# Third block of a fused network: conv sum split in two, and splits and value products reordered on VectorE and ScalarE

## The reference, cut to what matters

```python
z = rms_norm_2(x, mix_norm_g[l]) @ w_in[l]
(q, kc, vc, ks, vs, kw, vw, gl, zg, zc) = _split_cols(z, IN_SPLITS)
y_nsa = nsa_mixer(q, kc, vc, ks, vs, kw, vw, gl, cmp_pe[l], cmp_w1[l], cmp_w2[l])
y_gmlp = gmlp_mixer(zg, gmlp_ln_g[l], gmlp_ln_b[l], gmlp_ws[l], gmlp_bs[l])
y_conv = conformer_conv_mixer(zc, conv_dw_w[l], conv_dw_b[l], conv_ln_g[l], conv_ln_b[l])
...
y = jnp.concatenate([rms_norm_2(y_nsa, g_nsa), rms_norm_2(y_gmlp, g_gmlp),
                     rms_norm_2(y_conv, g_conv)], axis=-1)
x = x + y @ w_out[l]
```

## Time and profile before

| what | value |
|---|---|
| median of 3 runs | 944.64 us (944.25 to 947.62) |
| time of the profiled execution | 944.2 us |
| its span on the core | 942.5 us |
| PE busy | 896.2 us (95%) |
| DVE busy | 639.0 us (68%) |
| ACT busy | 469.8 us (50%) |
| POOL busy | 166.8 us (18%) |
| mean granted clock | 0.993 |

### The profile page before, as it was taken

How to read it: one execution, slowest core, us unless ns; L and a number is a source line. 1 busy time by engine, 2 the same in 40 slices (tenths; PEclk the granted TensorE clock), 3 DMA queues, 4 the chain that set the end, 5 groups by cost and what they waited for, 6 DMA issues and landing times.

```text
span 942.5 us, 15274 instructions
## 1 busy us (share of the span) xinstructions
PE 896.2 (95%) x5692; PEld 806.4 (86%) x5692; DVE 639.0 (68%) x948; ACT 469.8 (50%) x734; POOL 166.8 (18%) x131
## 2 busy tenths in 40 slices
PE   4999999999998999999999999989999989999996
PEld 4888888888997888888888999978798889999995
DVE  3897777776555678777678687966653676656655
ACT  4854444444545565444444635435543564555442
POOL 2200000000000000000000579102000264444441
PEclk9999999999999999999999999979999999999999
DMA  9777666643431557666674764211444486656601
GB/s 304 210 204 206 192 201 195 188 153 116 151 136 46 164 179 238 201 186 188 186 221 135 175 178 156 90 46 67 134 179 134 126 254 201 191 178 172 196 23 45
DMA packets 187172, 154.27 MB, mean 164 GB/s; under 512 B 6337, under 2 KB 172445, under 8 KB 187117
## 3 DMA queue, kind: packets, MB, share of 16 engines
q1 hardware_dynamic: 185517, 149.19, 52.2%
q0 software_dynamic: 752, 2.39, 1.0%
q10 hardware_dynamic: 848, 1.92, 0.6%
HBM read 151.92 MB, written 1.05 MB: 162 GB/s over the span
## 4 chain that ended last, share of the span: by engine, by line
PE 78%; DVE 10%; ACT 5%; issue 3%; DMA 2%; POOL 2%; SPq 0%; DVEq 0%; ACTq 0%
PE bank L1722 16%; PE bank L1724 16%; PE bank L1723 16%; PE bank L1850 16%; PE bank L1852 8%; DVE wl L991 3%; ACT wh L562 2%; DMA raw<-in_pool_w 1%; PE bank L1814 1%; PE bank L1739 1%; DVE yc L1342 1%; PE bank L2339 1%; POOL st L1617 1%; DVE xhl L1000 1%; PE bank L2318 1%
## 5 line engine op out<-in xcount | busy, mean ns | idle before, releaser
L1850 PE MATMUL bank<-xhl,wh 128*128 128x512 f32 x672 | 235.0, 394 | 0.6 <-DVE wl L991 0.6
L1852 PE MATMUL bank<-xhl,wl 128*128 128x256 f32 x672 | 186.3, 277 | 0.0
L1850 PEld LDWEIGHTS bank<-xhl,wh 128*128 128x128 f32 x672 | 126.0, 187 | 29.9 <-DVE wl L991 0.8
L1722 PE MATMUL bank<-xhl,wh 128*128 128x256 f32 (+1 forms) x520 | 147.9, 285 | 0.8 <-DVE xhl L1250 0.7
L1724 PE MATMUL bank<-xhl,wl 128*128 128x256 f32 (+1 forms) x520 | 146.9, 283 | 0.0
L1723 PE MATMUL bank<-xhl,wh 128*128 128x256 f32 (+1 forms) x520 | 146.9, 283 | 0.0
L991 DVE TENSOR_TENSOR wl<-raw,wh 128x2048 fp32r<-128x2048 f32 (+5 forms) x53 | 114.0, 2160 | 45.1 <-ACT wh L562 45.0
L630 ACT ACTIVATE wh<-raw 128x2048 fp32r<-128x2048 f32 x57 | 109.2, 1916 | 55.8 <-PE bank L1852 52.4
L1852 PEld LDWEIGHTS bank<-xhl,wl 128*128 128x128 f32 x672 | 126.2, 188 | 1.8
L1617 POOL TENSOR_SCALAR st<-ss 128x1 f32<-128x1 f32 x18 | 10.9, 606 | 580.4 <-ACT junk L571 580.2
L1722 PE MATMUL bank<-dh,hh 128*128 128x512 f32 x264 | 103.5, 392 | 5.5 <-DVE hl L1111 5.5
(11 more groups left out here) (304 smaller groups left out, 1712.6 us busy)
## 6 DMA issues: line engine op xcount, KB each, us to landing
raw<-in_ffn_w_up SPq DMA_DIRECT2D x88, 512.0 KB, 6.0
draw<-in_ffn_w_down SPq DMA_DIRECT2D x66, 512.0 KB, 3.6
raw<-in_ffn_w_gate SPq DMA_DIRECT2D x44, 512.0 KB, 5.2
raw<-in_w_in SPq DMA_DIRECT2D x18, 512.0 KB, 4.8
raw<-in_xattn_wk SPq DMA_DIRECT2D x8, 512.0 KB, 4.6
raw<-in_mla_w_o SPq DMA_DIRECT2D x8, 512.0 KB, 4.1
raw<-in_xattn_wv SPq DMA_DIRECT2D x8, 512.0 KB, 4.6
raw<-in_w_out SPq DMA_DIRECT2D x8, 512.0 KB, 4.1
```

What stands on the lines that cost most here:

```text
L1722: pe.matmul(outp, a_hi, b_hi, start=start, stop=False, **kw)
L1850: pe.matmul(b[:, :].rearrange("p (a s) -> p a s", a=2), wh[ns][:, a:a + P], xhl[:, :, k, :], start=k == 0, stop=False, skip_group_check=True)
L1852: ins = pe.matmul(b[:, 0:SEQ], wl[ns][:, a:a + P], xh[:, k, :], start=False, stop=k == KD - 1, skip_group_check=True)
```

## The change

- The region of overlaid tiles grows by 608 bytes, and a tile `yd` (128x256) is new.
- DVE's taps 18 to 30 of row 1 go into `yd` instead of `yc[:, 1, :]`. Tap 18 is a multiply alone, and no longer waits for POOL. A new instruction, `conv_join`, adds `yd` to `yc[:, 1, :]` when both sums are complete, and TensorE's turn of `yc` waits for one more signal.
- The stretches of taps are cut at other places: `conv(26, 33)` for `conv(26, 30)`, `conv(33, 34)` for `conv(30, 31)`, `conv(34, 39)` for `conv(31, 36)`, `conv(39, 44)` and the join for `conv(36, 44)`.
- DVE does `vbd` ahead of these last taps, and the split of `wout2` behind the four gate products of gMLP (L1478).
- ACT copies `kcm` ahead of its rounding of `wout2`, and rounds `wout3` behind `nsa_pt(5, 1)`.
- DVE does `comp_add(1)` behind the four scalings, and the split of `wout3` behind the four tile splits.

```diff
-        REGION = 58688
+        REGION = 59296
...
+        yd = at_("yd", [P, SEQ])
...
             nsa_exp(3, 1)
-            after("z_u")
             act.wait_ge(cmp_mm, 2)
             act.wait_ge(kcm_zero, 1)
             for g in range(GROUPS):
                 rows_ = slice(g * DH, (g + 1) * DH)
                 ins = act.activation(kcm[rows_, g, :], bank[2][rows_, 64:64 + NCMP], ACT.Copy, scale=0.5)
             ins.then_inc(cmp_out, 1)
+            after("z_u")
...
-            after("mem6")
             nsa_pt(5, 0)
             act.wait_ge(cy_done, 1)
             y_squares(2, 768, 1024)
             nsa_pt(5, 1)
+            after("mem6")
             split_t(6, xh, C_MOUT, 0, range(4, KD))
...
-                    if k == 0:
+                    if (k, c) == (POOL_TAPS, 1):
+                        ins = dve.tensor_scalar(yd[:, :], hc[:, 1, k:k + SEQ], tap, None, ALU.mult)
+                    elif k == 0:
                         ins = dve.tensor_scalar(yc[:, 0, :], hc[:, 0, 0:SEQ], tap, col[:, C_CDB:C_CDB + 1],
                                                 ALU.mult, ALU.add)
                     else:
-                        if (k - 1, c) in VECTOR_TAPS:
-                            dve.wait_ge(cv_tap, VECTOR_TAPS.index((k - 1, c)) + 1)
-                        else:
-                            dve.wait_ge(cv_tap_pool, k)
-                        ins = dve.scalar_tensor_tensor(out=yc[:, c, :], in0=hc[:, c, k:k + SEQ], scalar=tap,
-                                                       in1=yc[:, c, :], op0=ALU.mult, op1=ALU.add)
+                        dve.wait_ge(cv_tap, VECTOR_TAPS.index((k - 1, c)) + 1)
+                        acc = (yc[:, 0, :], yd[:, :])[c]
+                        ins = dve.scalar_tensor_tensor(out=acc, in0=hc[:, c, k:k + SEQ], scalar=tap,
+                                                       in1=acc, op0=ALU.mult, op1=ALU.add)
                     ins.then_inc(cv_tap, 1)
+
+            def conv_join():
+
+                dve.wait_ge(cv_tap, len(VECTOR_TAPS))
+                dve.wait_ge(cv_tap_pool, POOL_TAPS)
+                dve.tensor_tensor(yc[:, 1, :], yc[:, 1, :], yd[:, :], ALU.add).then_inc(cv_tap, 1)
...
             nsa_max(1)
-            conv(26, 30)
+            conv(26, 33)
             dve.wait_ge(shifted, 64)
...
             after("z_kcvc")
-            conv(30, 31)
+            conv(33, 34)
...
             after("z_v")
-            conv(31, 36)
+            conv(34, 39)
...
             gelu_out(1)
-            after("z_u")
-            conv(36, len(VECTOR_TAPS))
             dve.wait_ge(cmp_mm, 2)
             dve.wait_ge(cmp_out, 1)
...
+            conv(39, len(VECTOR_TAPS))
+            conv_join()
 
             nsa_max(4)
...
+            after("z_u")
             n240 = NT * NSA_HEADS * NCMP
             dve.wait_ge(sc_mm, 1)
...
-            after("mem6")
-            for t in range(NT):
-                ins = comp_add(t)
-                ins.then_inc(comp_in, 1)
+            comp_add(0).then_inc(comp_in, 1)
             dve.sem_inc(y_nsa, 1)
             dve.wait_ge(y_rs, 1)
...
+            comp_add(1).then_inc(comp_in, 1)
             dve.wait_ge(comp_in, NT)
             acc_evict(1, 1).then_inc(y_nsa, 1)
             split_t(6, xh, xl, C_MOUT, 0, range(4, KD))
+            after("mem6")
...
-            pe.wait_ge(cv_tap, len(VECTOR_TAPS))
+            pe.wait_ge(cv_tap, len(VECTOR_TAPS) + 1)
```

## The result

The changed kernel took 937.26 us, the median of 4 runs (936.66 to 938.1), against 945.36 us for the kernel before (4 runs, 944.25 to 947.62). The ratio is 0.991 with a 95% interval of 0.9898 to 0.9923. That is faster by 8.1 us or 0.9%. The forecast was 936.2 us in a range of 934.8 to 939.4. The profiled execution took 936.66 us where the sum in the prediction said 935.9.

The account below looks back on a forecast made before the run. TensorE was taken as the bound, losing 3.84 us of stop and 4.8 of half clock (8.6); minus 0.5 for exps, plus 0.9 for the copy, minus 0.7 for `comp_add` gives 8.3, so 936.2 us, range 934.8 to 939.4.

Parts of the forecast that it names:

- The place: Third block, TensorE's stop at L2250's sixteen products: 3.84 us of stop plus 4.8 us of half clock, 8.6 us to win.
- the walk along the times: Start times followed engine by engine from `vbd` to TensorE's turn of `yn` at 638.5: a gain of 8.3 us.
- Five taps and the join: DVE behind `vbd`: taps 2.6 us, join 0.5 us, so `nsa_max(4)` starts at 617.2, 4.57 us sooner.
- The split of `wout2` behind the gate product: DVE from 619.7 to 621.9 (2.29 us): costs 0.15 us on DVE's side and nothing on TensorE's.
- The split of `wout3`: End of the block: ACT's copy of (5, 0) 8.9 us sooner, `comp_add` gives back 0.6 to 0.7, turn at 638.5.
- The cover: DVE's 2.71 us wait for POOL hides its 2.29 us split of `wout3`, with 0.4 us left.
- The early taps: Three more instructions ahead of DVE's shifted-`kvc` wait: 1.86 us in 1.63 us of idle, 0.23 late, taken as 0.1.
- The clock falls all the same: Rival, chance 0.07: half clock follows a shorter stop, at 620 or before 638.5; 5 us lost, 941.2 us.
- The stop only moves: Rival, chance 0.03: TensorE waits as long at the value products behind L2250, for exps behind `nsa_max(4)`; 940.1 us.
- The `comp_add` is hidden: Rival, chance 0.07: `y_rs` comes later than said or the `comp_add` overlaps; gain 8.9 to 9.2 us, 935.3 us.
- DVE stays the bound: Rival, chance 0.13: dearer taps beside POOL, hand-overs or no cover left; gain 6.5 to 7.5 us, 937.2 to 938.2.
- Slower: Rival, chance 0.02: lasting half clock after TensorE's longer idle before L1739 at 638.5; 951 us if it lasts 30 us.

Follow-up runs that it names:

- 5: The kernel before with 31 extra TensorE products ahead of its wait for `vbd`, nothing else changed: 943.8 us, ratio 0.9977.
- 4: The changed kernel with the part of `wout3` and the second `comp_add` put back in their old places: 938.78 us, ratio 0.9933.
- 7: The changed kernel measured again, twice, with no further change: 936.75 us (ratio 0.9896) and 936.07 us (ratio 0.9905).
- 6: The changed kernel with the split of `wout2` back ahead of `kcm` (ACT) and `vbd` (DVE): 944.1 us, ratio 0.9974.
- 8: The changed kernel with the second `comp_add` ahead of DVE's wait for POOL, as before: 938.43 us, ratio 0.9926.
- 1: The kernel before with only the taps part (`yd`, the join, the new cuts of the taps): 944.49 us, ratio 0.999.
- 10: The changed kernel with the small shifted `kvc` loads ahead of `wout2`: 936.55 us; the same with 11 extra TensorE products in the stop at 756 to 759 us: 936.49.
- 3: The kernel before with only ACT's rounding and DVE's split of `wout3` and the second `comp_add` moved: 943.65 us, ratio 0.9983.
- 2: The kernel before with `kcm` and `vbd` first and the split of `wout2` moved, all eight taps behind `vbd`, no `yd`: 941.34 us, ratio 0.9951.
- 9: As 8, but with the eight old taps behind `vbd`, no `yd`, none at the front: 940.35 us, ratio 0.9937.

## Why the prediction was right

**The place holds 8.6 us, 3.84 of stop and 4.8 of clock: right, and the size too.** The stop is gone and the windows from 618 us show 1.00. The products take 1.92 us (forecast 1.8). That the clock was a term of its own is shown by 5, where the products took 1.94 us with nothing else moved. The best check of the size is 4: `kvc` was on time in it, the clock did not fall in the mixer, and only the part of `wout3` is missing. TensorE's turn gains 646.79 - 638.76 = 8.0 us there; the walk along the times had 8.1 up to the copy. Over all runs the mean granted clock is 0.9916 in the kernel before (17 runs beside run 7) and 0.9967 in the changed one (12 runs), 0.0051 x 940 = 4.8 us. This is an upper bound, since not every stretch at half clock need hold up the path: runs of the kernel before with 0.990 took 946.4 us in the mean and those with 0.993 945.0, 1.4 us apart and not 2.8.

**Five taps and the join: right, the join a little dear.** Five taps took 2.56 us (2.6), the join 0.42 us where I took 0.5. The formula of the Trainium skill (VectorE: DVE Perf Modes, TRN2 errata), which the page gives as exact for N of 512 and 2048, puts it at an estimated 0.42 us for 256, and the trace agrees. `nsa_max(4)` is at 618.83 - 0.71 = 618.1 (617.2), `nsa_max(5)` at 624.4 (623.4). Both are 0.9 to 1.0 us late, which is the shifted `kvc` of that execution: in the second of 7, with it on time, they are at 617.3 and 623.5.

**The split of `wout2` behind the gate product: right, and the most important step.** It cost TensorE nothing, and without it (6) next to nothing of the place's 8.6 us is left in the median.

**The split of `wout3`: right result, by two errors that cancel.** The copy of (5, 0) is at 633.8 (632.85), `y_scaled` at 636.7 (636.6), the turn at 638.5 (638.5), released by the `comp_add`. On the way 0.8 to 0.9 us were lost to the late `kvc`, which the prediction had on time, and 0.7 us won on POOL's step, which it took as unchanged. That the turn came at the forecast 638.5 is luck; with `kvc` on time it came at 637.69. For the same reason the idle time ahead of the turn is 0.79 us and not 1.9. The price of 0.7 us for the `comp_add` was not a real one against the other order (8). The cover held: DVE waited another 0.72 us for POOL behind the split. The first product of `wout3` is at 645.78, 645.1 on the old scale (forecast 645), 0.9 us behind the split's end at 644.88, with no wait. The prediction took the row at 662.73 for the first use of `xq0`; it is the first product of `wout0`, which waits 0.20 us for its own split, as its counterpart at 655.20 waits 0.18. `xq0` is used later, so there was more slack than the 10 us, and nothing hangs on the slip. The turn's gain is 646.79 - (639.23 - 0.71) = 8.3 us, as forecast. The span shows 7.6, because the 0.71 us of the first load are in it.

**The early taps: right, though their sign was set off.** In 1, where `kvc` was on time, `fl` began at 589.20 with the offset row at 15.71, so at 588.71, 0.24 us later than before; the forecast had 0.23. In 4 and 8 it was 0.2 us, in 6 and in the second of 7 0.4 to 0.5. In the profile of the changed kernel they cost nothing, since the data came later still. The prediction had named a start more than 0.3 us after 588.47 as a sign of being wrong. It came true in all three profiles of the changed kernel: by 1.6 and 1.9 us through the late data, which the sign did not allow for, and by 0.4 us with no wait in front.

**The rivals.** *The clock falls all the same* came true now and then, in pieces. It never cost the 5 us that I gave it in the changed kernel, but up to 1.7 us in single executions, behind a stop of 0.92 us there and of 0.17 and 0.20 us in 10. In one of three profiles of the changed kernel it fell in the third block, so as a rough estimate it belongs in the sum as some 0.6 us in the mean, not as a case of 0.07. *The stop only moves* did not happen in the changed kernel, but 6 shows how near it lay, and that I priced it too mildly: 944.1 us instead of 940.1, because `nsa_max(4)` is then hardly sooner at all (620.99 against 621.77 on the old scale) and the clock falls twice more later on. *The `comp_add` is hidden* named a gain of 8.9 to 9.2 us, which the quiet execution has (9.1), but by another cause: the `comp_add` still releases TensorE there, and what was won is POOL's step. No row shows *DVE stays the bound* or *Slower*.

**What stays open.** Why the clock falls behind one short stop and not behind another of the same length, and why it stays down 10 us behind the old stop (before, 1, 3), 6.8 in 6 and 3.4 elsewhere. The stops may not be the whole of it: the sixteen products of 30 columns and the value products of 64 stand close to each of these stops in the mixer, and no run separates what they do from what the stop does.

## What to carry to other kernels

When a stop of the busiest engine is followed by half clock, count both, but ask for each what ends the wait behind it: here 4.8 us of clock were worth 2.2 alone (5) and all of it only with the next producer moved as well. Look for the longest instruction that stands ahead of the wanted one in each in-order engine and that nobody waits for; moving the split of `wout2` (2.3 us on DVE, 1.9 on ACT) was worth more than moving single taps. Parts that work on one wait don't add: 1.0 and 4.1 us alone were 6.7 together.

## What the runs showed that I had not expected

- A step of 0.20 us on POOL (128x4) took 0.88 us while DVE ran a subtract of 128x2048 with both inputs in SBUF. It took 0.88 in all profiles where the two met (before, 1, 2, 4, 5) and 0.20 in all where they did not (3, 6 to 10, the changed kernel). In each of the five it ended 0.06 to 0.07 us behind the end of DVE's subtract. The moved split meets POOL's next step in the changed kernel, which takes 0.41 us for 0.19 and again ends 0.05 us behind the split, at 644.93 (the row below); DVE waits for that one, but TensorE's turn behind it, at 648.50, has no wait. That POOL and DVE share interfaces to SBUF stands in the Trainium skill (GPSIMD Engine Reference, Specifications), and the rows agree; here it was POOL that was held up, and POOL was on the path.

```profile
644.52 0.41 POOL L1713 TENSOR_SCALAR lst<-lst 128x1 f32<-128x1 f32 x1 [7.12 <-ACT junk L920]
```

- The clock fell for 3.4 us behind stops of 0.17 and 0.20 us (10), 0.91 (5), 0.92 (7), 1.38 (2) and 1.40 us (9), and stayed at 1.00 behind 0.29 and 0.72 us in the changed kernel, 0.17 and 0.21 us in 8 and 4, and 1.02 us at 614.57 in 5. The stop of 2.5 us that ends between 757 and 767 us was followed by half clock in 2, 4, 5, 6, 8 and 9, and not in 1, 3, 7, the first of 10 and the kernels before and after.
- Four small loads (some 128 KB each) behind 1 MB in the same queue landed 4.1 to 5.7 us after their issue (medians of two), ahead of it in 2.7 to 2.9 us.
